# Two norms between two networks merged into one formula and moved into the first network's last group

## The reference, cut to what matters

```python
    x = x + (1 + gate2[:, None, :]) * ((val * jax.nn.silu(gte)) @ w_down[l])
    return rms_norm(x, g_final)            # EPS = 1e-6
...
    x = layer_norm(x, ln_emb_g, ln_emb_b)  # LN_EPS = 1e-5
    h = x @ w_in[l] + b_in[l]
...
    x = layer_norm(DN_ALPHA * x + mix, ln1_g[l], ln1_b[l])
```

## Time and profile before

| what | us |
|---|---|
| median of 3 runs | 3461.03 |
| lowest and highest run | 3449.89, 3462.54 |
| the profiled execution's own time | 3455.78 |
| its span, first to last instruction | 3453.7 |
| mean granted TensorE clock | 0.922 |

### The profile page before, as it was taken

The page is one execution under the profiler, slowest core; times in us unless marked ns, Lnnn a source line. Parts: engine busy times, 40 slices in busy tenths (PEclk is TensorE's granted clock), DMA queues, the critical chain, the costliest instruction groups (busy, mean ns, idle before and its releaser), DMA issues. The chain is left out here.

```text
span 3453.7 us, 41277 instructions
## 1 busy us (share of the span) xinstructions
PE 2973.0 (86%) x16093; PEld 2558.6 (74%) x16093; DVE 1861.7 (54%) x3018; ACT 1034.6 (30%) x1536; POOL 888.3 (26%) x302
## 2 busy tenths in 40 slices
PE   4979996799999999948568648889988899999996
PEld 3778995697888888737456646779868788888885
DVE  7627673555555455572289776874244633333335
ACT  5424443322221121211156344652131311111111
POOL 1213320212232232312021421221102233333334
PEclk9989996799999999978789878999999999999998
DMA  6723323401111111011222232130133111111111
GB/s 229 261 76 75 73 68 112 149 23 69 49 37 61 42 43 61 25 43 47 59 74 104 86 74 72 44 121 25 62 146 129 50 42 46 48 47 49 49 61 49
DMA packets 117927, 256.89 MB, mean 74 GB/s; under 512 B 52708, under 2 KB 74727, under 8 KB 104599
## 3 DMA queue, kind: packets, MB, share of 16 engines
q1 hardware_dynamic: 113335, 238.13, 20.9%
q10 hardware_dynamic: 3744, 13.63, 1.2%
q0 software_dynamic: 704, 3.15, 0.2%
HBM read 210.97 MB, written 47.06 MB: 75 GB/s over the span
## 5 line engine op out<-in xcount | busy, mean ns | idle before, releaser
L1186 PE MATMUL psum<-h_hi,w_hl 128*128 128x512 f32 x2432 | 753.1, 391 | 16.6 <-DVE ffn_relu L1600 12.8
L1175 POOL TENSOR_TENSOR w_hl<-w_raw,w_hl 128x2048 fp32r<-128x2048 f32 x65 | 324.2, 4987 | 866.3 <-ACT w_hl L1169 866.3
L1186 PEld LDWEIGHTS psum<-h_hi,w_hl 128*128 128x128 f32 x2432 | 457.7, 189 | 114.4 <-issue 18.4
L1203 PE MATMUL psum<-w_hl,ffn_a_hi 128*128 128x512 f32 x1600 | 498.6, 393 | 6.3 <-DVE residual L1418 6.3
L1186 PE MATMUL psum<-h_lo,w_hl 128*128 128x512 f32 x1216 | 474.6, 390 | 0.0
L621 PE MATMUL psum<-w_hl,h_hi 128*128 128x256 f32 (+1 forms) x2048 | 377.9, 287 | 25.2 <-POOL w_hl L584 14.5
L621 PE MATMUL psum<-h_hi,w_hl 128*128 128x512 f32 (+1 forms) x1088 | 324.8, 382 | 38.7 <-POOL h_lo L2768 19.1
L1203 PEld LDWEIGHTS psum<-w_hl,ffn_a_hi 128*128 128x128 f32 x1600 | 301.5, 189 | 73.1 <-DVE residual L1418 6.8
L621 PEld LDWEIGHTS psum<-w_hl,h_hi 128*128 128x128 f32 x2048 | 326.0, 196 | 26.6 <-POOL w_hl L584 15.1
L1169 ACT ACTIVATE w_hl<-w_raw 128x2048 fp32r<-128x2048 f32 x65 | 124.5, 1916 | 691.8 <-PE psum L1203 357.9
L1203 PE MATMUL psum<-w_hl,ffn_a_lo 128*128 128x512 f32 x800 | 314.0, 392 | 0.0
(11 more groups left out here) (334 smaller groups left out, 4906.7 us busy)
## 6 DMA issues: line engine op xcount, KB each, us to landing
w_raw<-in_w_up SPq DMA_DIRECT2D x38, 1024.0 KB, 4.7
w_raw<-in_w_down SPq DMA_DIRECT2D x27, 1024.0 KB, 4.9
ada_w<-in_w_ada ACTq DMA_DIRECT2D x26, 512.0 KB, 4.8
w_raw<-in_w_in_T SPq DMA_DIRECT2D x12, 1024.0 KB, 7.1
ada_w<-in_w_ada SPq DMA_DIRECT2D x22, 512.0 KB, 5.1
w_raw<-in_xa_wkv SPq DMA_DIRECT2D x8, 1024.0 KB, 5.2
out_src<-mix SPq DMA_DIRECT2D x16, 512.0 KB, 5.6
w_raw<-in_w_in_G SPq DMA_DIRECT2D x8, 648.0 KB, 5.2
```

The costliest lines, as they stand in the source:

```text
L1175: pool.tensor_tensor(self.k.w_lo[s][:, :], self.k.w_raw[s][:, :], self.k.w_hi[s][:, :].bitcast(F), ALU.subtract).then_inc(self.k.wsem["w_r ...
L1186: m = pe.matmul(k.bank[b][:, :], w[:, t * CW + f * P:t * CW + (f + 1) * P], h[:, t, half * 512:half * 512 + 512], start=t == 0 and w is w_ ...
L1203: m = pe.matmul(k.bank[4 + out % 4][:, :], a[f][:, tile * P:(tile + 1) * P], w[:, f * D + half * 512:f * D + half * 512 + 512], start=f == ...
```

## The change

With a root-mean-square norm r and a layer norm behind it, the first row factor cancels but for the epsilons. So `y = x * g_final` is made once per tile (GpSimd), its mean and variance are taken (VectorE), and the row's factor is 1 / sqrt(var(y) + LN_EPS * (mean(x^2) + EPS)), for which ScalarE squares and sums `x`. VectorE makes (y - mean) * ln_gain, ScalarE multiplies by the row factor. The shift enters as a column when the halves are written; `k.x` itself no longer has it, and out2 adds it with its bias row (`before=`). `norm` is gone with its two blocks. All of this stands in the program of the last group of `ffn_conv`, for tiles 0 to 3 between the adds. Two of four banks of chunk 0 and two of chunk 1 of in2T (the half of rows of tiles 0 to 3) are made there too, and `project` leaves them out. in2T's first chunk now uses slot 1, so all later projections up to out2 have their slots swapped. Some tiles share memory that was apart.

```diff
-def norm(k, name, kind, gain, shift, hh=None, hl=None, out=None, ahead=None, saved=()):
...
-    def early_products(self, pe, hh, hl, b):
+        self.begun[0] = 4
+
+    def early_products(self, pe, hh, hl, b, ch=0):
         assert self.halves_first and self.hh is hh and self.hl is hl
-        pe.wait_ge(*self.at("w_ready", self.s0, 1))
-        self.bank_products(pe, self.s0, b)
-        self.begun = b + 1
+        s = ch % 2 ^ self.s0
+        pe.wait_ge(*self.at("w_ready", s, ch // 2 + 1))
+        self.bank_products(pe, s, b)
+        self.begun[ch] = b + 1
...
-            for b in range(self.begun if isinstance(c, int) and c == 0 else 0, self.banks):
+            for b in range(self.begun.get(c, 0) if isinstance(c, int) else 0, self.banks):
...
-def ffn_conv(k, wt, w_up, w_down, conv, hh, hl, gate, grow):
+def ffn_conv(k, wt, w_up, w_down, conv, hh, hl, gate, grow, low_at, lin, g_final, ln_gain, ln_shift):
...
+        junk, ln_row = u[0][:, 1, :], u[0][:, 0, :]
...
+        units = [((0, 1, 2, 3), (t,)) for t in range(KT)] + \
+                [(tiles, (2 * j, 2 * j + 1)) for tiles in ((4, 5), (6, 7)) for j in range(4)]
+        unit_bank = lambda m: k.bank[m % 4 if m < KT else (2, 3, 6, 7)[m % 4]]
+        tokens = lambda tiles: slice(tiles[0] * P, (tiles[-1] + 1) * P)
+        part = lambda m, j: unit_bank(m)[:, j * len(units[m][0]) * P:(j + 1) * len(units[m][0]) * P]
+        added = lambda i: 16 * (G - 1) + 2 * i + 2
...
+                lin.early(sp, "load", 1)
+                sp.dma_start(scol[:, :], ln_shift.rearrange("(t p) -> p t", p=P), allow_slow_non_contiguous=True)\
+                  .then_inc(shift_in, 16)
+                sp.wait_ge(w_gated, 2 * G)
+                sp.dma_start(grow[:, :], rows(g_final)).then_inc(rows_in, 16)
+                sp.wait_ge(a_lo_done, NF1 - 1)
+                sp.dma_start(ln_row, rows(ln_gain)).then_inc(rows_in, 16)
+                lin.early(sp, "load", 2)
...
+                def turn_units(start, count):
+                    for m in range(start, start + count):
+                        tiles, blocks = units[m]
+                        pe.wait_ge(normed, tiles[-1] + 1)
+                        if m == 0:
+                            pe.wait_ge(up_out, 4 * NF1)
+                        elif m < KT:
+                            reached(pe, lo, m - 3)
+                        elif m < KT + 4:
+                            pe.wait_ge(lo, KT)
+                            pe.wait_ge(dn_out, 16 * G)
+                        else:
+                            pe.wait_ge(lo, m - 3)
+                        for j, t in enumerate(blocks):
+                            for at, i in enumerate(tiles):
+                                mm = pe.transpose(part(m, j)[:, at * P:(at + 1) * P], k.x[:, i, t * P:(t + 1) * P],
+                                                  k.ident[:, :])
+                        mm.then_inc(turned, 1)
+                turn_units(0, 8)
+                pe.wait_ge(lo, KT)
+                pe.wait_ge(dn_out, 16 * G)
+                lin.early_products(pe, hh, hl, 0)
+                lin.early_products(pe, hh, hl, 1)
+                turn_units(8, 4)
+                lin.early_products(pe, hh, hl, 0, 1)
+                turn_units(12, 4)
+                lin.early_products(pe, hh, hl, 1, 1)
...
+                act.wait_ge(dn_mm, 16 * (G - 1))
+                lin.early(act, "hi", 1)
+
+                def square(i):
+                    act.wait_ge(dn_out, added(i))
+                    reached(act, squared, i)
+                    act.activation(junk, k.x[:, i, :], ACT.Square, scale=D ** -0.5, accum_out=ms[:, i:i + 1])\
+                       .then_inc(squared, 1)
+
+                def root(p):
+                    act.wait_ge(var_done, p + 1)
+                    act.activation(std[:, 2 * p:2 * p + 2], mv[:, 2 * p:2 * p + 2, 1], ACT.Sqrt).then_inc(std_done, 1)
+
+                def scale(p):
+                    act.wait_ge(rstd_done, p + 1)
+                    for i in (2 * p, 2 * p + 1):
+                        act.activation(k.x[:, i, :], k.x[:, i, :], ACT.Copy, scale=rstd[:, i:i + 1]).then_inc(normed, 1)
+
+                def upper(start, count):
+                    for m in range(start, start + count):
+                        tiles, blocks = units[m]
+                        act.wait_ge(turned, m + 1)
+                        for j, t in enumerate(blocks):
+                            e = act.activation(hh[:, t, tokens(tiles)], part(m, j), ACT.Identity, bias=scol[:, t:t + 1])
+                        e.then_inc(hi, 1)
+                square(0)
+                square(1)
+                root(0)
+                square(2)
+                square(3)
+                scale(0)
+                square(4)
+                square(5)
+                root(1)
+                square(6)
+                square(7)
+                act.wait_ge(dn_mm, 16 * G)
+                lin.early(act, "hi", 2)
+                scale(1)
+                act.wait_ge(shift_in, 16)
+                upper(0, 8)
+                root(2)
+                scale(2)
+                root(3)
+                upper(8, 4)
+                scale(3)
+                upper(12, 4)
...
+                lin.early(pool, "lo", 1)
+                pool.wait_ge(rows_in, 32)
+                pool.wait_ge(dn_mm, 16 * (G - 1))
+                for i in range(NT):
+                    pool.wait_ge(dn_out, added(i))
+                    reached(pool, gained, i - 3)
+                    pool.tensor_tensor(y[i % 4][:, :], k.x[:, i, :], grow[:, :], ALU.mult).then_inc(times_g, 1)
+                lin.early(pool, "lo", 2)
...
-                        if isinstance(g, int) and g == G - 1 and o % 2 and o > 1:
-                            dve.wait_ge(dn_out, 16 * g + o - 1)
-                            k.x_stats(dve, tile - 1)
...
-                add_down(G - 1, range(16))
-                dve.wait_ge(dn_out, 16 * G)
-                k.x_stats(dve, NT - 1)
+
+                def last_add(*tiles):
+                    for i in tiles:
+                        add_down(G - 1, (2 * i, 2 * i + 1))
+
+                def stats(i):
+                    dve.wait_ge(times_g, i + 1)
+                    for h in range(2):
+                        e = dve.bn_stats(k.stats[:, i, 6 * h:6 * h + 6], y[i % 4][:, 512 * h:512 * h + 512])
+                    e.then_inc(stats_done, 1)
+                    dve.wait_ge(stats_done, i + 1)
+                    dve.bn_aggr(mv[:, i, :], k.stats[:, i, :]).then_inc(aggr, 1)
+
+                def variance(p):
+                    pair = slice(2 * p, 2 * p + 2)
+                    dve.wait_ge(squared, 2 * p + 2)
+                    dve.tensor_scalar(ms[:, pair], ms[:, pair], LN_EPS, LN_EPS * EPS, ALU.mult, ALU.add).then_inc(widened, 1)
+                    dve.wait_ge(widened, p + 1)
+                    dve.wait_ge(aggr, 2 * p + 2)
+                    dve.tensor_tensor(mv[:, pair, 1], mv[:, pair, 1], ms[:, pair], ALU.add).then_inc(var_done, 1)
+
+                def centred_gain(p):
+                    for i in (2 * p, 2 * p + 1):
+                        dve.scalar_tensor_tensor(out=k.x[:, i, :], in0=y[i % 4][:, :], scalar=mv[:, i, 0:1], in1=ln_row,
+                                                 op0=ALU.subtract, op1=ALU.mult).then_inc(gained, 1)
+                    dve.wait_ge(std_done, p + 1)
+                    dve.wait_ge(gained, 2 * p + 2)
+                    dve.reciprocal(rstd[:, 2 * p:2 * p + 2], std[:, 2 * p:2 * p + 2]).then_inc(rstd_done, 1)
+
+                def lower(start, count):
+                    for m in range(start, start + count):
+                        tiles, blocks = units[m]
+                        dve.wait_ge(hi, m + 1)
+                        for j, t in enumerate(blocks):
+                            dst = (slice(None), t, tokens(tiles))
+                            e = dve.scalar_tensor_tensor(out=hl[dst], in0=part(m, j), scalar=scol[:, t:t + 1],
+                                                         in1=hh[dst].bitcast(F), op0=ALU.add, op1=ALU.subtract)
+                        e.then_inc(lo, 1)
...
+                last_add(0, 1, 2)
+                dve.wait_ge(rows_in, 32)
+                dve.wait_ge(shift_in, 16)
+                stats(0)
+                last_add(3)
+                stats(1)
+                variance(0)
+                last_add(4, 5)
+                centred_gain(0)
+                last_add(6)
+                stats(2)
+                stats(3)
+                variance(1)
+                last_add(7)
+                centred_gain(1)
+                lower(0, 8)
+                for p in (2, 3):
+                    stats(2 * p)
+                    stats(2 * p + 1)
+                    variance(p)
+                    centred_gain(p)
+                lower(8, 8)
+                dve.wait_ge(lo, 16)
...
-                lin_T1 = Linear(k, d["w_in2_T1"], 3, "T", hh, hl)
```

(8 more changed lines are left out.)

191 lines of the change are left out of this document (24 added, 167 removed).

## The result

The changed kernel takes 3395.67 us in the median of 4 runs (3392.60 to 3407.47), the kernel before 3456.59 beside it (3449.89 to 3462.54). The ratio is 0.9832, with a 95% interval of 0.9807 to 0.9856: by it, 58 us less, 50 to 67. A gain of 45 us was forecast; the median lies 4.3 us under the range given.

A forecast was written before the change was run, and what follows sets the result against it. TensorE bounds the kernel, losing 69.67 us in the gap before in2T. Less 10 waiting, 8.6 and 3.8 for transposes and 2.04 border, 44.9 us are gained: 3455.78 becomes 3410.9, written 3413 for scatter; range 3400 to 3432.

The forecast's parts named there:

- Up to 1492.24, where the third tile has its last add, nothing changes: Start of the expected course: until that add in the first network's last group, the timeline stays as before.
- TensorE's last down product ends within 1 us of 1505.5: Sign at the first network's end: TensorE finishes its products near 1505.45, as before.
- border: Switch between two blocks before in2T's last eight banks: priced at 2.04 us, bounds 0.7 to 2.04.
- No pause before units 8 and 12: Sign in the transposes: second-half tiles are scaled under early banks, so TensorE pauses no more than 1 us there.
- Ten us of waiting: Between last down product and first transposes: TensorE waits 10 us until tile 3 is normed at 1515.5.
- two variances, estimated 0.4: Term in VectorE's work for tiles 0 to 3: the small variance instructions cost 0.4 us of 18.6.
- Adds no more than 4 us behind their product: Sign in the last group: an add over 4 us behind its product would prove the forecast wrong.
- No centring held: VectorE's centrings beside GpSimd's gain products: collisions cost 0, at worst 4.9 us; over 2 us each would disprove it.
- Clock low after turning: Rival, 10%: after transposes, early banks three and four also start at the low clock; 3419, at most 3433 us.
- Chain longer in the last group: Rival, 15%: adds fall behind in the engines' fixed orders and a product waits, 5 to 12 us; 3418 to 3425.
- given back later: Rival, 3%: in2T ends early but its successor finds a load or split missing; 3455 us.
- slower: Rival, 2%: fixed orders of ScalarE, VectorE and GpSimd lock step, hiding nothing under products; 96.5 for 69.7, 3482 us.

The follow-up runs named there:

- a_shift: Changed kernel with 64 unused bytes ahead of a_hi, so it lies 64 bytes past a multiple of 128 again; median 3406.1 us, ratio 0.9868.
- a_again: Changed kernel run once more without any edit, for a second trace and more times; median 3398.5 us, ratio 0.9841.
- a_no_early: Changed kernel with the four early banks of in2T moved from between the transposes to behind them; median 3416.3 us, ratio 0.9901.
- a_bias_root: Changed kernel with ms given to ScalarE's root as its bias, dropping VectorE's small addition to the variance; median 3395.4 us, ratio 0.9835.
- a_adds_first: Changed kernel with all sixteen last adds on VectorE put ahead of the first tile's statistics; median 3405.0 us, ratio 0.9855.
- a_round_late: Changed kernel with ScalarE's rounding of the projection's second chunk moved behind the scaling of tiles 2 and 3; median 3396.6 us, ratio 0.9836.
- a_warm: Changed kernel with 36 unused products on TensorE between the last down product and the first transpose; median 3401.0 us, ratio 0.9842.
- a_best: Changed kernel with ms as the root's bias, the second chunk's rounding behind the scaling, and 24 unused products in TensorE's wait; median 3401.3 us, ratio 0.9840.
- a_two: Changed kernel with ms as the root's bias and the second chunk's rounding behind the scaling of tiles 2 and 3; median 3393.7 us, ratio 0.9828.

## Why the prediction was wrong

**The step that failed** is the first of the forecast's course: "Up to 1492.24, where the third tile has its last add, nothing changes", and with it "TensorE's last down product ends within 1 us of 1505.5". It holds for the order of instructions, and I took it to hold for their lengths. The change gives 960 of the 1,056 down products another place for their stationary operand, and in the long runs each is 6.7 ns shorter. This term was 0 in the sum. The last down product came 7.1 us earlier (1498.34), and a_shift, which moves nothing but the place back, has a first network 7.4 us longer than a_again. With the operand at its old offset the change is worth 0.9868, 45.6 us with an interval of 40 to 51, and the median is 3406.1: that is the forecast's 44.9, and inside its range. No rival had this in it, nor had the bounds.

The median came 17.3 us under the 3413 that I wrote. Of these, 7.1 lie ahead of the change (all but some 0.7 by the place, as shown above), 2.5 in the stage, and 2.1 what I had added for the scatter of runs. For the other 5.6 there is only that scatter.

**The mechanism** was right for the stage itself, and its terms came out as follows:

| term of the sum | forecast | measured |
|---|---|---|
| waiting for the first scaled tiles | 10.0 | 9.56 |
| first 32 transposes with their evacuation | 8.6 | 8.11 |
| two early banks | 12.69 | 12.65 |
| 16 transposes and a bank, first | 7.35 | 7.22 |
| 16 transposes and a bank, second | 7.35 | 7.36 |
| border | 2.04 | 0.48 |
| the last eight banks | 43.5 | 43.77 |

All in all the stage gave 2.4 us more than 44.9, and 1.6 of them are the border, which came out below both its bounds (0.7 and 2.04).

**Point by point.**

- *No pause before units 8 and 12*: right, and a_no_early shows what it is worth, 17 us.
- *Ten us of waiting*: right in size, in part by luck. My terms for VectorE add up to 1511.8, not to the 1512.3 that I wrote. GpSimd was idle when the centrings started, as I had it (its products ended at 1491.86 and 1501.23, the centrings began at 1494.18 and 1502.57). But its product held a VectorE instruction that I had priced inside "two variances, estimated 0.4" for 2.31 us. ScalarE was still last by its rounding, but by 0.4 us and not 1.0, and moving the rounding away won 0.3. Most of the hold was covered: in a_bias_root it turned into waiting for products.
- *Adds no more than 4 us behind their product*: barely. Product 9 ended near 1488.2, and its add began at 1491.80, 3.6 late. TensorE stood for 0.2, and the last group took 22.7 us where it took 22.2 in a_bias_root and a_adds_first, without the hold.
- *No centring held*: right, two took 2.47.
- *Clock low after turning* (10%): no. The 16 transposes behind a bank took 1.91 us, at a granted clock of 1.00:

```profile
1528.66:1530.57 1.91, 1.91 (x18) 1.91 (x17) 0.40 (x2) 1.27 (x4) 0.00 (x0) 1.00 0.00 0
```

The Trainium skill (TensorE: Matmul & The Clock Gate, "Part 4: PE-mode transpose") has it that the full rate does not engage for transposes; this trace doesn't agree.

- *Chain longer in the last group* (15%), *given back later* (3%), *slower* (2%): none. The offset at in2N, 54.5 us, is still 55.1 at the window attention.

**What is open.** The median gain, 58 us, is 3.5 above the stage and the 7.1 ahead of it together. Runs of one kernel scatter by 12 us or more, through stick breaking and window attention, and a_again gave 0.9841, 55 us, which the two explain. Six traces with the change have the grant fall in the first bank (after, a_again, a_shift, a_round_late, a_adds_first, a_warm), and three do not (a_bias_root, a_best, a_two: those with ms as the root's bias). Why wasn't settled.

## What to carry to other kernels

An edit that adds or drops buffers can change the speed of code that it doesn't touch: list where the stationary operands of long runs of matmuls lie before and after, and test with pads of several sizes, since the first one here, 64 bytes, gave next to nothing; a multiple of 256 bytes was 3% on these products. Work done under a last group of products, and products put between transposes, are worth what they cover (8 and 17 us here); price each by putting it back. On VectorE, small instructions with operands in SBUF are priced by what GpSimd does beside them, not by their size.
